# A two-layer decoder step on one core: state updates ahead of a split, two half strips at a layer's end, rounded sample scores, and where ada_w blocks are eaten

## The reference

```python
for i in range(DEPTH):
    mod = silu(c) @ ada_w[i] + ada_b[i]
    sh1, sc1, g1, sh2, sc2, g2 = jnp.split(mod, N_ADA, axis=-1)
    h = rmsnorm(x, norm_mix_g[i]) * (1.0 + sc1[:, None]) + sh1[:, None]
    if i % N_MIXERS == 0:
        out, s = retention(h, pos0, ret_state[j], ret_w_in[j], ret_gn_g[j], ret_w_out[j], chunk)
    else:
        out, s = pool_mixer(h, pool_state[j], pool_hist_len, pool_w[j], pool_scale[j])
    x = x + g1[:, None] * out
    h = rmsnorm(x, norm_ffn_g[i]) * (1.0 + sc2[:, None]) + sh2[:, None]
    x = x + g2[:, None] * swiglu(h, ffn_w_in[i], ffn_w_out[i])
```

## Time and profile before

| | |
|---|---|
| time, median of 3 runs | 3372.54 us (3367.27 to 3377.86) |
| the profiled execution | 3371.44 us, its span 3369.6 us |
| PE busy | 3277.1 us (97%) |
| DVE busy | 1714.7 us (51%) |
| ACT busy | 1072.8 us (32%) |
| POOL busy | 135.3 us (4%) |
| mean granted PE clock | 0.981 of full |
| DMA | 701.14 MB, 208 GB/s on average |

### The profile page before, as it was taken

How to read it: one execution, slowest core, us unless ns; L and a number is a source line. 1 busy time by engine, 2 the same in 40 slices (tenths; PEclk the granted TensorE clock), 3 DMA queues, 4 the chain that set the end, 5 groups by cost and what they waited for, 6 DMA issues and landing times.

```text
span 3369.6 us, 54480 instructions
## 1 busy us (share of the span) xinstructions
PE 3277.1 (97%) x23627; PEld 3063.4 (91%) x23627; DVE 1714.7 (51%) x2660; ACT 1072.8 (32%) x1286; POOL 135.3 (4%) x174
## 2 busy tenths in 40 slices
PE   7999999999999989999999999999899999999998
PEld 4788898989889978999999999998799999999998
DVE  4335464545646466444444444445845555555554
ACT  2232322323222324233232232234433333333334
POOL 0000000000000011000000000002200000000001
PEclk7899999999999999999999999998899999999999
DMA  9885867668676567766677776674244444444443
GB/s 331 274 288 189 271 207 259 227 221 269 204 265 197 177 203 251 246 237 238 238 245 245 248 244 233 237 241 148 88 151 150 150 149 149 149 150 149 150 150 106
DMA packets 505008, 701.14 MB, mean 208 GB/s; under 512 B 21149, under 2 KB 427102, under 8 KB 504441
## 3 DMA queue, kind: packets, MB, share of 16 engines
q1 hardware_dynamic: 483136, 619.26, 55.6%
q0 software_dynamic: 20544, 75.02, 6.8%
q10 hardware_dynamic: 1090, 3.39, 0.3%
HBM read 656.11 MB, written 41.48 MB: 207 GB/s over the span
## 4 chain that ended last, share of the span: by engine, by line
PE 91%; DVE 4%; DMA 3%; ACT 1%; issue 0%; POOL 0%; ACTq 0%; SPq 0%; DVEq 0%; POOLq 0%
PE pair L1424 79%; PE adab L1437 4%; DMA sb_raw<-in_ada_w 2%; PE m L1404 1%; DVE sb_big L1238 1%; DVE sb_w_lo L904 1%; PE m L1688 1%; PE m L1654 1%; DMA sb_big<-in_ada_w 1%; DMA sb_o_s<-in_ada_w 1%; PE pair L1404 0%; DVE sb_X L1021 0%; PE adab L1541 0%; PE m L1684 0%; PE m L1541 0%
## 5 line engine op out<-in xcount | busy, mean ns | idle before, releaser
L904 DVE TENSOR_TENSOR sb_w_lo<-sb_raw,sb_w_hi 128x1024 fp32r<-128x1024 f32 x792 | 966.4, 1223 | 1192.5 <-ACT sb_w_hi L613 1186.2
L613 ACT ACTIVATE sb_w_hi<-sb_raw 128x1024 fp32r<-128x1024 f32 x792 | 837.9, 1059 | 1920.2 <-PE pair L1424 1597.6
L1424 PE MATMUL pair<-sb_h_hi,sb_w_hi 128*128 128x320 f32 x4480 | 1040.5, 314 | 16.5 <-DVE sb_h_lo L1003 7.3
L1424 PE MATMUL pair<-sb_h_lo,sb_w_hi 128*128 128x320 f32 x4480 | 1024.5, 310 | 0.0
L1424 PE MATMUL pair<-sb_h_hi,sb_w_lo 128*128 128x320 f32 x4480 | 1024.4, 310 | 0.0
L1424 PEld LDWEIGHTS pair<-sb_h_hi,sb_w_hi 128*128 128x128 f32 x4480 | 750.3, 189 | 46.6 <-issue 38.5
L1424 PEld LDWEIGHTS pair<-sb_h_lo,sb_w_hi 128*128 128x128 f32 x4480 | 753.1, 189 | 0.0
L1424 PEld LDWEIGHTS pair<-sb_h_hi,sb_w_lo 128*128 128x128 f32 x4480 | 752.4, 189 | 0.0
L1424 PE MATMUL pair<-sb_y_hi,sb_w_hi 128*128 128x320 f32 x1856 | 428.5, 312 | 3.2 <-DVE sb_y_lo L1226 3.2
L1424 PE MATMUL pair<-sb_y_lo,sb_w_hi 128*128 128x320 f32 x1856 | 423.5, 309 | 0.0
L1424 PE MATMUL pair<-sb_y_hi,sb_w_lo 128*128 128x320 f32 x1856 | 423.4, 309 | 0.0
(11 more groups left out here) (256 smaller groups left out, 1501.3 us busy)
## 6 DMA issues: line engine op xcount, KB each, us to landing
sb_raw<-in_ffn_w_in SPq DMA_DIRECT2D x352, 512.0 KB, 3.6
sb_raw<-in_ret_w_in SPq DMA_DIRECT2D x192, 512.0 KB, 6.1
sb_big<-in_ada_w SPq DMA_DIRECT2D x181, 512.0 KB, 4.8
sb_raw<-in_ffn_w_out SPq DMA_DIRECT2D x176, 512.0 KB, 3.5
sb_raw<-in_ada_w SPq DMA_DIRECT2D x112, 512.0 KB, 5.3
sb_big<-in_state_ret POOLq DMA_DIRECT2D x32, 1024.0 KB, 8.3
sb_raw<-in_ret_w_out SPq DMA_DIRECT2D x64, 512.0 KB, 3.6
out_state_ret_sample<-sb_big POOLq DMA_DIRECT2D x32, 1024.0 KB, 5.8
```

Source lines behind the costliest of these rows:

```text
L613: A(w_hi[s][:, :, :], raw[slot][:, :, :], ACT.Copy).then_inc(hi_done, 1)
L904: V.tensor_tensor(w_lo[s][:, :, :], raw[slot][:, :, :], w_hi[s][:, :, :].bitcast(F32), ALU.subtract)\
L1424: ins = MM(pair[p][:, m, 0:T], w[s][:, k, P * m:P * m + P], x[:, c, :], start=first and k == 0 and n == 0, stop=last and k == BK - 1 and n ...
```

## The change

1. **State updates.** `update(0)` of an out lap goes ahead of DVE's fourth split of that lap (it was behind it); in the last head it goes ahead of the fourth split of its written-out list.
2. **Sample scores.** `probs_s` is of the rounded type; DVE's `step_C` weighs the scores in one instruction into `weighed`, casts them to `probs_s` and subtracts to get a low part. `step_E` runs two rounded matmuls over 512 columns for each of the two rows of sequences, where there was one in fp32.
3. **Groups and eights.** `HEAD_GROUPS` is 6 (was 7); there are 28 eights (were 26), at gemms 6, 12, 18, 24, and from 30 on every 9 or 10; the last is due at gemm 254.
4. **Layer ends.** `ff_end` computes the first halves of strip 0 and of strip 1 (into two other PSUM banks, `spare`), then the second halves; DVE's `residual(1)` reads `spare`.
5. **norm(2) and the pool loop.** `turn_history` stands behind the spread. `low_m(0)` and `low_m(2)` stand behind the third window's work.
6. **Preload.** `first_gemm(4)` and `fold_pre(6)` stand right behind block 55 (were behind block 63 and block 59); DVE does two of its splits ahead of `mod_pre(6)`.

```diff
-GROUPS, HEAD_GROUPS, MOD_PRE = 20, 7, 2 * PRE_STRIPS
-FF_FIRST, EIGHT_FROM, EIGHT_EVERY, EIGHTS = H * 32, 6, 10, 2 * (GROUPS - HEAD_GROUPS)
+GROUPS, HEAD_GROUPS, MOD_PRE = 20, 6, 2 * PRE_STRIPS
+FF_FIRST, EIGHTS = H * 32, 2 * (GROUPS - HEAD_GROUPS)
+EIGHT_AT = [6 + 6 * e if e < 4 else 30 + (e - 4) * 39 // 4 for e in range(EIGHTS)]
...
-            eights = [4 + b // 2 if b < 4 else 8 if b < 8 else EIGHT_EVERY * (b // 8) + 4 + b % 8 for b in range(8 * EIGHTS)]
+            eights = [4 + b // 2 if b < 4 else 8 if b < 8 else EIGHT_AT[b // 8] - 2 + b % 8 for b in range(8 * EIGHTS)]
...
+            split(), split()
             mod_pre(6)
-            split(), split()
...
-                V.tensor_tensor(probs_s[:, 0, :], mbank[0][:, 0:P], decay[:, TP:], ALU.mult)
-                V.tensor_tensor(probs_s[:, 1, :], mbank[0][:, P:2 * P], decay[:, TP:], ALU.mult).then_inc(dv["C"], 1)
+                V.tensor_tensor(weighed, mbank[0][:, 0:2 * P].rearrange("p (r n) -> p r n", r=2),
+                                decay[:, TP:].unsqueeze(1).broadcast_to([P, 2, P]), ALU.mult).then_inc(dv["C"], 1)
+                dve.wait_ge(dv["C"], C("head"))
+                then(V.tensor_copy(probs_s[:, :, :], weighed))
+                settle()
+                V.tensor_tensor(low[:, 0:2 * P].rearrange("p (r n) -> p r n", r=2), weighed, probs_s[:, :, :].bitcast(F32),
+                                ALU.subtract).then_inc(probs_split, 1)
...
-                posts[3] = ([lambda: update(0), taken] + posts[3]
-                            + [lambda: update(1)])
+                posts[2] = [lambda: update(0), taken]
+                posts[3] = posts[3] + [lambda: update(1)]
...
-                for _ in range(4):
+                for _ in range(3):
                     split()
                 update(0)
                 taken()
+                split()
...
                 posts[3] = [lambda: finish_up(1)] + posts[3]
+                posts[4] = [lambda: residual(1, mod, G2, apart=True)]
...
-                if c % 4 == 0:
+                if c == 4:
+                    low_m(0)
+                    low_m(2)
+                if c % 4 == 0 or g == 0:
                     continue
                 low_m(c - 2)
-                if g == 0:
-                    low_m(c)
-                    continue
...
-                if n == 2:
-                    turn_history()
                 pe_.wait_ge(n_diag, n + 1)
...
                 ins.then_inc(n_rb, 1)
+                if n == 2:
+                    turn_history()
...
-                      51: lambda: fold_pre(5), 59: lambda: fold_pre(6)}
+                      51: lambda: fold_pre(5), 55: lambda: (first_gemm(4), fold_pre(6))}
...
             fold_pre(7)
-            first_gemm(4)
             first_gemm(5)
...
                 pe_.wait_ge(dv["D"], C("head"))
+                pe_.wait_ge(probs_split, C("head"))
...
-                    MM(mbank[r][:, :], probs_s[:, r, :], vs_tok[:, r, :].bitcast(F32), start=True, stop=False, skip_group_check=True)
+                    for i, part in enumerate((probs_s[:, r, :], low[:, P * r:P * r + P])):
+                        MM(mbank[r][:, :], part, vs_tok[:, r, :], start=i == 0, stop=False, skip_group_check=True)
...
-                s = C.n["gemm"] % SPLIT_SLOTS
-                pe_.wait_ge(lo_done, C("gemm", 1))
-                pe_.wait_ge(pair_free[0], C("strip", 0, 2))
-                products(s, 0, (0, 1), range(4), True, False, y_hi, y_lo)
-                pe_.wait_ge(pair_free[1], C("strip", 0, 2))
-                products(s, 0, (2, 3), range(4), False, True, y_hi, y_lo).then_inc(gemm_done, 1)
-                C.n["gemm"] += 1
-                C.n["strip"] += 1
-                eights_beside()
-                lap4(first=1)
+                slots = [(C.n["gemm"] + i) % SPLIT_SLOTS for i in range(2)]
+                for half in range(2):
+                    pe_.wait_ge(pair_free[half], C("strip", 0, 2))
+                    for i, p in enumerate((0, None)):
+                        if not half:
+                            pe_.wait_ge(lo_done, C("gemm", 1 + i))
+                        ins = products(slots[i], p, (2 * half, 2 * half + 1), range(4), half == 0, half == 1, y_hi, y_lo)
+                        if half:
+                            ins.then_inc(gemm_done, 1)
+                C.n["gemm"] += 2
+                C.n["strip"] += 2
+                lap4(first=2)
```

More of the change, by code:

```diff
@@ L137, in eight_due @@
 def eight_due(gemms, late=0):
-    e, rest = divmod(gemms - FF_FIRST - EIGHT_FROM - late, EIGHT_EVERY)
-    return e if rest == 0 and 0 <= e < EIGHTS else None
+    n = gemms - FF_FIRST - late
+    return EIGHT_AT.index(n) if n in EIGHT_AT else None
 def group_at(n):
@@ L206, in decoder_step @@
         probs = sb("probs", [P, TP + P])
[L207 removed]
+        probs_s = sb("probs_s", [P, 2, P], F32R)
         k_tok = sb("k_tok", [P, 2, DK])
@@ L276, in decoder_step @@
         last_sums = [adab[:, :], pair[0][:, 0, :], pair[0][:, 1, :]]
+        spare = [mbank[0][:, 0:T], mbank[2][:, 0:T]]
         four = [mbank[0], mbank[1], mbank[2], adab]
@@ L1013, in modulate, with residual @@
                 low(len(UNITS) - 1)
-            def residual(s, gate, chunk, back=-LOOK_OUT):
+            def residual(s, gate, chunk, back=-LOOK_OUT, apart=False):
                 j = s % 2
+                src = spare if apart else [pair[j][:, c, 0:T] for c in range(2)]
                 caught_up()
@@ L1020, in residual @@
                 for c in range(2):
-                    V.scalar_tensor_tensor(X[:, 2 * s + c, 0:TP], pair[j][:, c, 0:TP],
+                    V.scalar_tensor_tensor(X[:, 2 * s + c, 0:TP], src[c][:, 0:TP],
                                            gate[:, chunk + 2 * s + c, 0:1], X[:, 2 * s + c, 0:TP], ALU.mult, ALU.add)
-                then(V.tensor_tensor(samples(sample_tmp[:, j, :, :]), samples(pair[j][:, :, TP:T]),
-                                     by_token(gate, chunk + 2 * s, 2), ALU.mult))
+                for c in range(2):
+                    if apart:
+                        last = V.tensor_tensor(samples(sample_tmp[:, j, c:c + 1, :]), samples(src[c][:, TP:T].unsqueeze(1)),
+                                               by_token(gate, chunk + 2 * s + c, 1), ALU.mult)
+                if not apart:
+                    last = V.tensor_tensor(samples(sample_tmp[:, j, :, :]), samples(pair[j][:, :, TP:T]),
+                                           by_token(gate, chunk + 2 * s, 2), ALU.mult)
+                then(last)
                 settle()
@@ L1174, in step_A, with step_C @@
                 V.tensor_tensor(probs[:, TP:], mbank[0][:, TP:TP + P], decay[:, 0:P], ALU.mult).then_inc(dv["A"], 1)
[L1176 removed]
+            def step_C(low=y_lo[:, 0, :]):
                 caught_up()
                 dve.wait_ge(pe["C"], C("head"))
[L1179 to L1180 removed]
+                V.tensor_tensor(weighed, mbank[0][:, 0:2 * P].rearrange("p (r n) -> p r n", r=2),
[5 more added lines that the diff above has]
+                                ALU.subtract).then_inc(probs_split, 1)
             def group_norm(step, to, which):
@@ L1280, in _ @@
                 head(last=h == H - 1)
-            step_A(), step_C(), step_D()
+            step_A(), step_C(h_lo[:, 8, :]), step_D()
             split()
@@ L1418, in products @@
             def products(s, p, ks, chunks, first, last, hi=h_hi, lo=h_lo):
+                to = [pair[p][:, m, 0:T] for m in range(2)] if p is not None else spare
                 for k in ks:
@@ L1676, in step_D, with step_E @@
                 prompt_state(1).then_inc(pe["D"], 1)
-            def step_E():
+            def step_E(low=y_lo[:, 0, :]):
                 pe_.wait_ge(dv["D"], C("head"))
+                pe_.wait_ge(probs_split, C("head"))
                 for i in range(4):
@@ L1754, in _ @@
             out_strip()
-            step_E()
+            step_E(h_lo[:, 8, :])
             out_strip()
```

6 lines of the change are left out of this document (3 added, 3 removed).

## The result

The changed kernel takes 3354.88 us (median of 5 runs, 3350.86 to 3356.28) where the kernel before takes 3372.54 (5 runs beside it, 3367.27 to 3378.89): 17.7 us less, a ratio of 0.9946 with a 95% interval of 0.9934 to 0.9958. The forecast was 3353.5. The profiled execution of the changed kernel took 3356.28 us, span 3354.4, and was the longest of the five; against the profiled execution of before it is 15.2 us shorter.

A forecast was written before the change was run, and what follows sets the result against it. The prediction took TensorE (PE), 91% of the chain of waits, as the bound. Its terms -7.6 - 6.2 - 5.7 - 2.4 + 3.9 - 1.0 gave -19.0, so 3353.5 us on the median, range 3345 to 3364.

The forecast's parts named there:

- Part 1: Out laps of the heads: PE's state products stop waiting for DVE's state updates, -7.6 us (bounds -8.7 and -0.7).
- Part 2: step_E: four rounded records at an estimated 236 ns replace four of 0.43 us, 0.78 per head, -6.2 us.
- Part 3: A group of ada_w blocks leaves head 6 (13.3 us) for two eights and a fold in feed-forward 0 (7.6): -5.7 us.
- Part 4: Layer ends: shorter wait and upper clock gain in layer 1, layer 0 loses 1.1 us; together -2.4 us.
- Part 5: norm(2): history turned behind the spread delays ACT's copies and then its modulation, which PE waits for, +3.9 us.
- (a): Pool stage: the moved history costs nothing, as ACT's copies are caught up in idle time; 3349.6 us, chance 0.16.
- Part 6: Preload: gemm 4 fills a 3.26 us wait of PE, partly paid back before gemm 6, -1.0 us.
- (b): Out lap: DVE is full and the removed wait returns at a later update or residual; 3360.4 us, chance 0.10.
- (c): step_E: a rounded matmul over 512 columns costs a record's 0.43 us; +6.2, 3359.7 us, chance 0.06.
- (d): Feed-forward 0: eights six gemms apart hold SP, delaying weight loads queued behind; 3381.8 us, chance 0.06.

The follow-up runs named there:

- low_m_back: The changed kernel with low_m(0) and low_m(2) back where they stood; norm(2) to norm(3) took 78.45 us, against 76.86 in the changed kernel.

## Why the prediction was right

The sum was -19.0 and the median moved by -17.7; the two halves of the sum that carry it, heads and groups, came out term by term. That the two agree to 1.3 us is in part luck: the five runs of the changed kernel span 5.4 us, and the terms of the pooling mixer and of the preload are no larger than the scatter of their stretches.

**Part 1 (-7.6)**: shown. The wait of the state products is 1.1 us instead of 8.7 (2.5 in the update's own run, with the 1.4 of the last head), and the update alone shortens seven heads by 0.74 to 1.60, 8.0 in all. The reason given holds too: it is the place in DVE's queue, and DVE had 1.60 us of idle to use at that point.

**Part 2 (-6.2)**: shown, 0.78 in step_E itself and 0.85 per head alone, against 0.78. A rounded record of 512 columns is 230 ns; scaling by columns gave 236. The extra DVE work is hidden: the only wait in front of step_E is one in the last head, for a step before it, 0.79 before and 0.78 after.

**Part 3 (-5.7)**: head 6 is 15.15 shorter, of which 13.2 is left when the 1.92 of the parts 1 and 2 is taken off. In feed-forward 0 the matmuls of eights and folds take, from start to start, 105.59 us where they took 98.05: 7.5 more, where 7.55 was forecast for two eights and a fold. Net -5.7. No wait took its place.

**Part 4 (-2.4)**: -3.19 in layer 1 and about +1.2 in layer 0 (8.73 less the 7.5 of the eights), together -2.0. The clock's part, which the prediction took as 1.7, is 1.4.

**Part 5 (+3.9)**: +3.4 by the profiled pair. Six profiles with the history ahead have 71.65 to 76.12 us (mean 73.5), five with it behind 76.53 to 78.45 (mean 77.1): 3.6. These stretches end in the scatter that low_m_back met, and three of the six have the old low_m order, so the cleaner figure is taken ahead of both: from norm(2)'s first sum to the start of `turn_new_history` the six take 11.2 to 12.7 us (mean 11.9) and the five 15.3 to 16.2 (mean 15.9), 4.0 apart, with nothing between. Rival (a) falls.

**Part 6 (-1.0)**: the step that is only half right. The wait of 3.26 is gone, and gemm 6 starts at 132.75, 0.8 earlier than before, but not by the way that was reckoned. Three things were not in the sum. Gemm 4 runs partly at the lower clock where it now stands (24 matmuls from 112.29 to 117.66, 5.4 us, where 3.54 was reckoned). The blocks loaded later are waited for 2.0 us in all. And gemm 5 runs partly at the lower clock too (4.9 us from 127.02), so that a wait of 0.69 is left before gemm 6 where 2.0 was forecast. In the end the gain is about 0.9 in the mean of the profiles, inside a scatter of 3: the term's size is not shown, and its closeness to -1.0 is luck.

The rivals: (a) and (b) are refuted by the runs above, (c) by the 230 ns of a record, (d) by a harder test than the change makes.

The profiled execution's -15.2 against a median of -17.7 fits with the stretches that scatter: of the seven profiles with the changed preload none has a later first step_A than the changed kernel's own, 209.60, and of the 12 profiles none has a longer stretch from the eighth step_A to norm(1) than the changed kernel's own, 79.00, and the shortest has 74.86.

## What to carry to other kernels

When an engine works strictly in its own order, read what stands ahead of the late instruction in that queue and what that waits for: moving an update past one waiting split was worth 1.1 us per lap and cost nothing. The other way round, work that fills a wait on the chain (the history's transposes) must stay there, even if the instruction behind it gets its input a little later, since its reader may be the next link. Differences of a few microseconds in 3,350 are decided by stretches between fixed instructions, not by totals, and even then by several profiles, because a single stretch can scatter by three or four.
